# RWKV right-hand sides and y products in 128x64 column tiles, column turns as whole blocks, and x in front of the first loads

## What is computed

```python
def wkv7(r, w, k, v, a, b):                  # (B,T,H,N), H = 16 heads, N = 64
    def step(S, inp):
        r_t, w_t, k_t, v_t, a_t, b_t = inp
        sa = jnp.einsum('bhvk,bhk->bhv', S, a_t)
        S = S * w_t[:, :, None, :] + sa[..., None] * b_t[:, :, None, :] + v_t[..., None] * k_t[:, :, None, :]
        y = jnp.einsum('bhvk,bhk->bhv', S, r_t)
        return S, y
```

## Time and profile before

| | us |
|---|---|
| median of 3 runs | 1437.56 (1437.47 to 1438.98) |
| the profiled execution | 1436.71 |
| its span, first to last instruction | 1434.8 |
| PE busy in the span | 1384.1 (96%) |
| DVE / ACT / POOL busy | 857.3 / 697.0 / 38.2 |
| chain that ended last: PE's share | 88% |

### The profile page before, as it was taken

How to read it: one execution, slowest core, us unless ns; L and a number is a source line. 1 busy time by engine, 2 the same in 40 slices (tenths; PEclk the granted TensorE clock), 3 DMA queues, 4 the chain that set the end, 5 groups by cost and what they waited for, 6 DMA issues and landing times.

```text
span 1434.8 us, 22841 instructions
## 1 busy us (share of the span) xinstructions
PE 1384.1 (96%) x8466; PEld 1135.2 (79%) x8466; DVE 857.3 (60%) x1236; ACT 697.0 (49%) x1104; POOL 38.2 (3%) x41
## 2 busy tenths in 40 slices
PE   6999999999999999999899999999999998999998
PEld 5888877778788778888777688777888887788887
DVE  4545568875655464455866677656555576465554
ACT  5434446665465453344544343235444466454442
POOL 0000000000000000000000000110000020000000
PEclk9999999999999999999899999999999999999999
DMA  8655545555444565555443001314555741255552
GB/s 278 222 176 175 177 139 194 169 181 189 160 157 167 147 198 197 176 175 176 140 161 112 22 3 32 109 43 157 182 190 178 240 156 41 78 188 187 182 190 103
DMA packets 145516, 220.40 MB, mean 154 GB/s; under 512 B 16753, under 2 KB 65151, under 8 KB 145313
## 3 DMA queue, kind: packets, MB, share of 16 engines
q1 hardware_dynamic: 145440, 219.36, 46.8%
HBM read 218.26 MB, written 1.05 MB: 153 GB/s over the span
## 4 chain that ended last, share of the span: by engine, by line
PE 88%; DVE 5%; ACT 4%; issue 1%; POOL 0%; DMA 0%; SPq 0%; ACTq 0%; DVEq 0%
PE gp L289 12%; PE gp L290 12%; PE gp L291 12%; PE acc L289 12%; PE acc L291 12%; PE acc L290 11%; PE gp L2653 2%; PE tp L906 1%; PE acc L2668 1%; ACT sb_xa_hi L453 1%; DVE sb_w_lo L278 1%; ACT sb_w_hi L262 1%; ACT sb_arena L403 1%; PE tp L289 1%; PE acc L2625 1%
## 5 line engine op out<-in xcount | busy, mean ns | idle before, releaser
L278 DVE TENSOR_TENSOR sb_w_lo<-sb_raw,sb_w_hi 128x1024 fp32r<-128x1024 f32 (+1 forms) x380 | 452.1, 1215 | 226.8 <-ACT sb_w_hi L262 225.1
L262 ACT ACTIVATE sb_w_hi<-sb_raw 128x1024 fp32r<-128x1024 f32 (+1 forms) x380 | 388.2, 1053 | 221.1 <-PE acc L291 107.6
L289 PE MATMUL gp<-sb_w_hi,sb_xa_hi 128*128 128x512 f32 (+1 forms) x752 | 301.7, 401 | 12.0 <-DVE sb_xa_lo L460 9.8
L290 PE MATMUL gp<-sb_w_hi,sb_xa_lo 128*128 128x512 f32 (+1 forms) x752 | 294.1, 391 | 0.0
L291 PE MATMUL gp<-sb_w_lo,sb_xa_hi 128*128 128x512 f32 (+1 forms) x752 | 294.0, 391 | 0.0
L289 PEld LDWEIGHTS gp<-sb_w_hi,sb_xa_hi 128*128 128x128 f32 x752 | 142.9, 190 | 45.2 <-issue 10.8
L291 PEld LDWEIGHTS gp<-sb_w_lo,sb_xa_hi 128*128 128x128 f32 x752 | 142.9, 190 | 30.3
L290 PEld LDWEIGHTS gp<-sb_w_hi,sb_xa_lo 128*128 128x128 f32 x752 | 143.2, 190 | 27.4 <-issue 0.5
L289 PE MATMUL acc<-sb_w_hi,sb_mid_hi 128*128 128x512 f32 x408 | 159.1, 390 | 0.0
L291 PE MATMUL acc<-sb_w_lo,sb_mid_hi 128*128 128x512 f32 x408 | 158.9, 389 | 0.0
L290 PE MATMUL acc<-sb_w_hi,sb_mid_lo 128*128 128x512 f32 x408 | 158.7, 389 | 0.0
(11 more groups left out here) (410 smaller groups left out, 1778.8 us busy)
## 6 DMA issues: line engine op xcount, KB each, us to landing
sb_raw<-in_ffn_w SPq DMA_DIRECT2D x264, 256.0 KB, 4.3
sb_raw<-in_mlp_w SPq DMA_DIRECT2D x256, 256.0 KB, 2.9
sb_raw<-in_w_in SPq DMA_DIRECT2D x72, 256.0 KB, 3.1
sb_raw<-in_a_w_rkv SPq DMA_DIRECT2D x48, 256.0 KB, 4.1
sb_raw<-in_xattn_w_kv SPq DMA_DIRECT2D x32, 256.0 KB, 3.4
sb_raw<-in_w_out SPq DMA_DIRECT2D x16, 256.0 KB, 2.9
sb_raw<-in_xattn_w_q SPq DMA_DIRECT2D x16, 256.0 KB, 3.0
sb_raw<-in_xattn_w_o SPq DMA_DIRECT2D x16, 256.0 KB, 3.0
```

What stands on the lines that cost most here:

```text
L262: A.e.activation(w_hi[:, s, :, 0:n], raw[:, r, :, 0:n], ACT.Copy).then_inc(hi_done, 1)
L278: V.e.tensor_tensor(w_lo[:, s, :, 0:n], raw[:, r, :, 0:n], w_hi[:, s, :, 0:n].bitcast(F32), ALU.subtract).then_inc(lo_done, 1)
L289: e.matmul(dst, xh, wh, start=start, stop=False)
L290: e.matmul(dst, xl, wh, start=False, stop=False)
```

## The change

- **Column tiles.** pe_rhs and the y products of pe_y are issued as pairs of matmuls, each with 64 of the 128 stationary columns, to the two halves of the output partitions. The halves are crossed() as elsewhere: stationary columns `at` go to output partitions `at`. The state update stays as it was.
- **Column turns.** pe_columns turns slot 7 in one 128x128 transpose against a new constant, `crossed`, an identity rolled by 64 columns. The half turns, their semaphore and the wait on it are gone. The constant makes the second constants DMA 64 KB longer.
- **The start.** SP issues the first tile of x, then ident, then the gain of ffn1's pre norm alone (8 rows), then the chunks. The ten gain vectors follow behind chunk 5, in front of the other constants. PE turns the 8 rows at the start and the others in ffn1 after the second pe_turn_first (aside); they go through acc instead of gp, so the first down products wait for ACT's copies.

```diff
 put("ident", eye)
+put("crossed", np.roll(eye, HALF, 1))
...
 # FeedForward.pe
                 self.pe_turn_first(T, 1)
+                if aside is not None:
+                    aside()
                 self.pe_up_token(T, 1, 1, range(0, 4))
...
 # FeedForward.lane
                 upto(L, self.start(1) + self.ups)
+                if aside is not None:
+                    aside()
                 out(L, 0)
...
 # SetUp
             def sp(self, sp):
+                self.rows_in(sp, 0)
                 sp.dma_start(ident, a["consts"][:, 0:P]).then_inc(consts_loaded, 16)
+                sp.dma_start(first_gain, a["ffn1_pre_g"].rearrange("a (k p) -> (a k) p", p=P)).then_inc(first_gain_loaded, 16)
+
+            def sp_vectors(self, sp):
...
-                self.rows_in(sp, 0)
...
             def pe(self, T):
                 T.e.wait_ge(consts_loaded, 16)
+                T.e.wait_ge(first_gain_loaded, 16)
+                T.e.transpose(gp[:, 0, 0:8], first_gain, ident[0:8, 0:8]).then_inc(*T.one(first_gain_turned))
+
+            def pe_vectors(self, T):
...
-                T.e.transpose(gp[:, 0, 0:n], gain_rows[0][0:n, :], ident[0:n, 0:n]).then_inc(*T.one(gains_turned))
+                T.e.transpose(acc[:, 0, 0:n], gain_rows[0][0:n, :], ident[0:n, 0:n]).then_inc(*T.one(gains_turned))
...
 # TimeMix.pe_columns
-                def half_turn(j, at, there):
-                    return T.e.transpose(self.stream_banks(s)[2 + j][:, there], self.pair_rows(7, t, g, j)[at, :], ident[at, at])
-
                 for j in range(2):
-                    half_turn(j, *self.crossed()[j]).then_inc(*T.one(self.half_turned))
-                for j in range(2):
-                    for n, slot in enumerate((4, 2, 5), 1):
-                        T.e.transpose(self.stream_banks(s)[2 + j][:, n * P:(n + 1) * P], self.pair_rows(slot, t, g, j), ident)
-                    T.e.wait_ge(self.half_turned, 2 * u + j + 1)
-                    half_turn(j, *self.crossed()[1 - j]).then_inc(*T.one(self.turned))
+                    for n, slot in enumerate((7, 4, 2, 5)):
+                        mm = T.e.transpose(self.stream_banks(s)[2 + j][:, n * P:(n + 1) * P], self.pair_rows(slot, t, g, j),
+                                           const("crossed") if n == 0 else ident)
+                    mm.then_inc(*T.one(self.turned))
...
 # TimeMix.pe_rhs
                     if t:
-                        T.e.matmul(tp[:, s, j * P:(j + 1) * P], self.fm[i % 2][s][:, j, 0, :], self.s_buf[:, 2 * g + j, :], start=True, stop=True)
+                        for at, there in self.crossed():
+                            T.e.matmul(tp[at, s, j * P:(j + 1) * P], self.fm[i % 2][s][:, j, 0, at], self.s_buf[:, 2 * g + j, :], start=True, stop=True)
                     for m in (2 * j, 2 * j + 1):
-                        mm = T.e.matmul(tp[:, s, m * HD:(m + 1) * HD], self.mt[s][:, m, 2, :], self.head_rows(6, t, g, m), start=t == 0, stop=True,
-                                        skip_group_check=t > 0)
+                        for at, there in self.crossed():
+                            mm = T.e.matmul(tp[at, s, m * HD:(m + 1) * HD], self.mt[s][:, m, 2, at], self.head_rows(6, t, g, m), start=t == 0, stop=True,
+                                            skip_group_check=t > 0)
...
 # TimeMix.pe_y (the state's products for t = 1 are split in the same way)
                     for m in (2 * j, 2 * j + 1):
-                        dst = tp[:, s, m * HD:(m + 1) * HD]
-                        T.e.matmul(dst, self.mt[s][:, m, 3, :], self.head_rows(6, t, g, m), start=t == 0, stop=False, skip_group_check=t > 0)
-                        mm = T.e.matmul(dst, self.mt[s][:, m, 1, :], self.u_buf[s][:, m, :], start=False, stop=True, skip_group_check=t > 0)
+                        for at, there in self.crossed():
+                            T.e.matmul(tp[at, s, m * HD:(m + 1) * HD], self.mt[s][:, m, 3, at], self.head_rows(6, t, g, m), start=t == 0, stop=False,
+                                       skip_group_check=t > 0)
+                        for at, there in self.crossed():
+                            mm = T.e.matmul(tp[at, s, m * HD:(m + 1) * HD], self.mt[s][:, m, 1, at], self.u_buf[s][:, m, :], start=False, stop=True,
+                                            skip_group_check=t > 0)
...
 # the blocks of SP, ACT, DVE and PE
-            ffn1.sp(sp, lambda: setup.rows_in(sp, 1), lambda: (setup.sp_rest(sp), ffn1_post.sp(sp)))
+            ffn1.sp(sp, lambda: setup.rows_in(sp, 1), lambda: (setup.sp_vectors(sp), setup.sp_rest(sp), ffn1_post.sp(sp)))
...
-            ffn1.act(A, ffn1_post)
+            ffn1.act(A, ffn1_post, lambda: setup.act_vectors(A))
+            A.e.wait_ge(gains_ready, 2)
...
             ffn1.dve(V, ffn1_post)
+            V.e.wait_ge(gains_ready, 2)
...
-            ffn1.pe(T, ffn1_pre, lambda t: (x_loaded[t], 16))
+            ffn1.pe(T, ffn1_pre, lambda t: (x_loaded[t], 16), (gains_ready, 2), lambda: setup.pe_vectors(T))
```

More of the change, by code:

```diff
@@ L69 @@
 for _n, _w in (("ident", 128), ("cos", 64), ("sin", 64), ("causal", 384), ("invalid", 384), ("dist", 384), ("tri", 129),
-               ("ends", 2), ("upper", 512), ("pair", 128), ("ident64", 64)):
+               ("ends", 2), ("upper", 512), ("pair", 128), ("ident64", 64), ("crossed", 128)):
     CONSTS[_n] = (_at, _w)
@@ L917, in pe_turn_first, with pe @@
                         mm.then_inc(self.mid_turned, 1)
-            def pe(self, T, pre, h_ready, acc_free=None):
+            def pe(self, T, pre, h_ready, acc_free=None, aside=None):
                 pre.turn.pe_token(T, 0, h_rows, h_ready(0))
@@ L938, in pe, with lane @@
                 self.pe_tail(T)
-            def lane(self, L, upto, one, first, middle, out):
+            def lane(self, L, upto, one, first, middle, out, aside=None):
                 upto(L, self.c0 + self.ups)
@@ L976, in dve_out_token, with act @@
                 V.e.tensor_tensor(lo, turned, hi.bitcast(F32), ALU.subtract).then_inc(self.tail_cols, 1)
-            def act(self, A, post=None):
-                self.lane(A, split_hi, self.hi_one, self.act_first, self.act_middle, lambda L, i: self.turn_out(L, i, True))
+            def act(self, A, post=None, aside=None):
+                self.lane(A, split_hi, self.hi_one, self.act_first, self.act_middle, lambda L, i: self.turn_out(L, i, True), aside)
                 i = self.trips - 1
@@ L1030, in build @@
         gains_turned = sem("gains_turned")
+        first_gain = rows(7)[0:8, 0, 2 * P:3 * P]
+        first_gain_loaded, first_gain_turned, first_gain_ready = sem("first_gain_loaded"), sem("first_gain_turned"), sem("first_gain_ready")
         class SetUp:
             def sp(self, sp):
+                self.rows_in(sp, 0)
                 sp.dma_start(ident, a["consts"][:, 0:P]).then_inc(consts_loaded, 16)
+                sp.dma_start(first_gain, a["ffn1_pre_g"].rearrange("a (k p) -> (a k) p", p=P)).then_inc(first_gain_loaded, 16)
+            def sp_vectors(self, sp):
                 vectors = [("ffn1_pre", a["ffn1_pre_g"]), ("mix_pre", a["mix_pre_g"]), ("mem", a["mem_g"]),
@@ L1057, in pe, with act_vectors @@
                 T.e.wait_ge(consts_loaded, 16)
+                T.e.wait_ge(first_gain_loaded, 16)
+                T.e.transpose(gp[:, 0, 0:8], first_gain, ident[0:8, 0:8]).then_inc(*T.one(first_gain_turned))
+            def pe_vectors(self, T):
                 T.e.wait_ge(gains_loaded, 160)
                 n = GAIN_SPLIT
-                T.e.transpose(gp[:, 0, 0:n], gain_rows[0][0:n, :], ident[0:n, 0:n]).then_inc(*T.one(gains_turned))
-                T.e.transpose(gp[:, 0, n:n + 48], gain_rows[1][0:48, :], ident[0:48, 0:48]).then_inc(*T.one(gains_turned))
+                T.e.transpose(acc[:, 0, 0:n], gain_rows[0][0:n, :], ident[0:n, 0:n]).then_inc(*T.one(gains_turned))
+                T.e.transpose(acc[:, 0, n:n + 48], gain_rows[1][0:48, :], ident[0:48, 0:48]).then_inc(*T.one(gains_turned))
             def act(self, A):
+                A.e.wait_ge(first_gain_turned, 1)
+                A.e.activation(gains[:, 0:8], gp[:, 0, 0:8], ACT.Copy).then_inc(*A.one(first_gain_ready))
+                A.e.wait_ge(*A.last)
+            def act_vectors(self, A):
                 A.e.wait_ge(gains_turned, 2)
                 n = GAIN_SPLIT
-                A.e.activation(gains[:, 0:n], gp[:, 0, 0:n], ACT.Copy).then_inc(*A.one(gains_ready))
-                A.e.activation(gains[:, GAINS["mu"]:GAINS["mu"] + 48], gp[:, 0, n:n + 48], ACT.Copy).then_inc(*A.one(gains_ready))
-                A.e.wait_ge(*A.last)
+                A.e.activation(gains[:, 8:n], acc[:, 0, 8:n], ACT.Copy).then_inc(*A.one(gains_ready))
+                A.e.activation(gains[:, GAINS["mu"]:GAINS["mu"] + 48], acc[:, 0, n:n + 48], ACT.Copy).then_inc(*A.one(gains_ready))
             def dve(self, V):
                 V.e.wait_ge(consts_loaded, 16)
-                V.e.wait_ge(gains_ready, 2)
+                V.e.wait_ge(first_gain_ready, 1)
```

5 lines of the change are left out of this document (3 added, 2 removed).

## The result

The changed kernel takes 1422.91 us (median of 4 runs, 1420.05 to 1423.98), the kernel before 1437.51 (4 runs, 1436.78 to 1438.98): ratio 0.9896, 95% interval 0.9873 to 0.9919. Its profiled execution took 1423.15 us with a span of 1421.2.

What follows compares the result with a forecast made beforehand. PE was taken to bound the RWKV core, with DVE not far behind. From 1436.71 us, 8.4 for the core and 0.3 for the start were subtracted: 1428.0, or 1428.9 on the median's scale; range 1424.5 to 1434.0.

Steps and rivals of the forecast that it cites:

- Behind them stand the post gain and chunks 6 to 9: Start: loads queued behind vectors, constants and levels come hardly earlier, so 0.6 of 3.9 us head start is left.
- The bounds, -1.5 and 3.9: Start: limits of its gain in us, 3.9 if nothing behind is late, about -1.5 if PE idling lowers its clock.
- The price of a record, 0.031 us: Right-hand sides and y: spacing of the new 64-column matmul records, taken from step z's 64x64 tiles, two halves in turn.
- the other bound of 0.112: Right-hand sides and y: upper limit in us per new record, if two halves never overlap and nothing gets shorter.
- the change of tile shape: Core: switching tile shape costs 0.20 us behind the right-hand sides before and after; one more in y adds 0.09.
- only 0.3 of 0.96 arrives: Unit 5: DVE runs group norm almost without break up to its masks, 0.31 us idle, so most gain is lost.
- The bonus chain of DVE: Unit 7: after y(6) gives 0.4 us, this DVE work is late.
- Rival D: Core as forecast, but a PE clock fall at the start or on busier work later: 1.7 us less, 1430.6; chance 0.15.
- A: Start: the whole head start stays because loads behind the vectors land in time, 3.6 us more gain, 1425.3; chance 0.07.
- B: Core: column halves take turns rather than overlap, 0.062 us a record, 1437 to 1438 us; chance 0.07.
- C: Core: no overlap and no shorter load, 0.112 us a record, +15 us, about 1452; chance 0.04.
- E: Core gives about half, through unseen ACT and DVE waits or halves spaced at 0.045: 4 us less, 1433; chance 0.12.

Runs made afterwards that it cites:

- the vectors behind the levels: Changed kernel with SP issuing the other constants and level masks right behind chunk 5, the ten gain vectors after them: 1421.24 us, ratio 0.9885.
- the core alone: Kernel before with the column tiles and whole column turns, but its own old start: 1423.44 us, ratio 0.9899.
- the hold: SP waits ahead of the MLP's first weight loads until seven units have their y; on the changed kernel 1420.19 us, on the kernel before 1434.92 us.
- the tiles alone: Kernel before with column tiles in right-hand sides and y only, half turns and start as before: 1428.10 us, ratio 0.9933.

## Why the prediction was wrong

The direction and the price of a column record were right, two terms were too small, and a third effect was not in the sum. Of the 6.0 us between forecast and measurement, 1.8 are the start and 2.7 the core; the rest is put down to stretches at a low clock.

**The start: forecast 0.3 us, measured 2.1** (2.3 over all profiles). What held: the head start (first product at 10.17, 3.5 us earlier), the issue of the constants (17.38, forecast 16.96), two turns aside at 0.37 us for 0.3. The step that failed is "Behind them stand the post gain and chunks 6 to 9", with chunk 7 at perhaps 30.4 and DVE's wait at about 4. I carried the time from the issue of the constants to the landing of the levels over from the old kernel (17.14 to 25.93, 8.8 us). In the new one it is 6.1 (17.38 to 23.46). The DMAs had run empty before it, which fits, but the vectors behind the levels keep them from being the whole reason. DVE waits 1.93 us, chunk 7 is there at 28.29, PE has it at 30.66 for the 32.75 forecast. How PE loses its head start can be read step by step: its lead is 3.49 us at the first product, 2.86 at 29.16, after waits for low parts of 0.63 (at 25.60) and 0.54, 2.61 at 31.00, and 2.12 at 32.76, behind the two turns. The bounds, -1.5 and 3.9, held it; the value taken was too low.

**The core: forecast 8.4 us, measured 11.1** (read in the core alone, against the profile of before, from masks to masks; the forecast's terms add up to 8.3, as 7 x 0.36 is 2.5 and not 2.6):

| stretch | forecast | measured |
|---|---|---|
| first turns and unit 0 | 0.75 | 1.3 |
| units 1 to 4 | 5.3 | 6.25 |
| units 5 and 6 | 1.0 | 1.8 |
| unit 7 and the last y | 1.3 | 1.7 |

- The price of a record, 0.031 us, was right (0.031 and 0.030). The neighbour with 64x64 tiles was the row to take, not the other bound of 0.112.
- Rhs gave 0.42 for 0.36, y 0.75 for 0.58, the turns 0.39 for 0.38 (1.56 a unit less the two others; measured alone, the turns gave 0.49 and the tiles 1.06). The mis-sized term is the change of tile shape: I kept it at 0.20 and added 0.09 in y; behind the new tiles the next step follows their last record in 0.14 (852.84 less 852.70), and the added change costs nothing that can be seen. That is 0.06 twice and the 0.09, 0.21 of the 0.24 us missing per unit (1.56 for 1.32).
- Ahead of unit 0 PE is the bound, so the first turns give 0.7 and not 0.4: no ACT copy stands in the way there, as products of the weights fill in.
- In unit 5 "only 0.3 of 0.96 arrives" failed. It read DVE's idle time in front of the masks alone. DVE is idle 1.45 us more ahead of the first merge behind them, and that slack passes the gain on: timeline of DVE before, and at the same step in the core alone:

```profile
900.87 0.44 DVE L2915 COPY_PREDICATED sb_arena<-sb_levels,acc 128x256 f32<-128x256 uint8 x1 [1.45 <-PE acc L2668]
```

```profile
889.41 0.44 DVE L2917 COPY_PREDICATED sb_arena<-sb_levels,acc 128x256 f32<-128x256 uint8 x1 [0.56 <-PE acc L2664]
```

- In unit 6 nothing of the turns and y arrives behind that step, as forecast: from it to the masks of unit 7 both kernels take 10.1 us (900.87 to 910.97, 889.41 to 899.50), with POOL's power and the scaling in front.
- In unit 7 y(6) and the last y were given 0.4 and 0.5, beside 0.36 for rhs(6); 1.1 arrive with rhs(6) and y(6), whose steps give 0.42 + 0.75, and 0.6 with the last y. The bonus chain of DVE isn't late.

**Outside the sum.** The two profiled executions differ by 13.6 us: 2.1 from the start, 11.1 from the steps of the core, 1.6 from a fall of the clock at 797 that only the old one of the two has, less 1.9 for the longer stop of PE near 906 with the fall behind it (against the core alone), and 0.6 from falls elsewhere (1.0 less 1.6 and 0.2 ahead of the core, plus 1.4 behind it; rounded). Rival D had a price of 1.7 for such a fall, and one of them did come, at 909; it didn't weigh that the kernel before has falls too, which a change can just as well take away. The medians differ by 14.6, so some 1.4 us beyond the two terms are put down to such stretches, in the mean over executions; which of them the change itself moves is open, beyond the counts given above.

**The rivals.** A (the whole head start stays, 3.6 more) was as far off as the forecast, which had 0.3 where 2.1 came; B and C are refuted by the records; of E nothing was seen.

## What to carry to other kernels

When a transfer is moved, its landing can't be had from its issue plus the old difference: the levels took 8.2 us from issue to landing in the kernel before, 5.6 in the one after, and an issue 3.5 us earlier brought 0.3; look at the windows of DMA share ahead of it. When a step of an engine becomes shorter, follow its gain past the first wait to the next idle stretch of the other engine before writing it off. And where instructions are small and many, keep bulk loads out of that stretch: here they delayed what PE needed next, and four of the ten stops had a stretch at 1.2 GHz right behind them.

## What the runs showed of the hardware

- Two fp32 column halves of 128x64 overlap fully: 0.057 us a record alone, 0.030 in turn, 0.118 for the whole 128x128 tile.
- With bulk loads at some 400 GB/s a 16 KB packet on the instruction queue started 1.9 us late; PE stood for 0.44 to 1.79 us in all ten profiles without the hold and not at all in the four with it.
- What follows such a stop differs: nothing behind 0.44 to 0.76 us, nothing behind one of 1.45 either (the tiles alone), 3.4 us at a granted clock of 0.50 behind 1.02, 1.03 and 1.31, and 20.5 us behind 1.79. What sets the length is open.
